# Experts worked on in the order of their number of chunks, sorted on VectorE, and a scatter that GpSimd waits for one step later

## The reference

```python
def moe_ffn(x, w_router, router_bias, w_gate, w_up, w_down):
    gates = group_limited_router(x2d, w_router, router_bias)      # 2 of 16 experts for each token
    y = jnp.zeros((bsz * t, d), jnp.float32)
    for e in range(N_EXPERTS):
        he = jax.nn.silu(x2d @ w_gate[e]) * (x2d @ w_up[e])
        y = y + gates[:, e:e + 1] * (he @ w_down[e])
    return y
x = layer_norm(DN_ALPHA * x + moe_ffn(x, ...), ln_ffn_g[l], ln_ffn_b[l])
```

## Time and profile before

| | us |
|---|---|
| median of 3 runs (lowest, highest) | 971.27 (966.42, 971.51) |
| profiled execution | 970.41 |
| its span, first to last instruction | 968.6 |
| TensorE busy | 890.6 |
| mixture of experts, layer 0 and layer 1 (first product of a chunk to the first of `add_choices`) | 200.6 to 469.3 and 680.3 to 941.3 |

### The profile page before, as it was taken

The page is one execution under the profiler, slowest core; times in us unless marked ns, Lnnn a source line. Parts: engine busy times, 40 slices in busy tenths (PEclk is TensorE's granted clock), DMA queues, the critical chain, the costliest instruction groups (busy, mean ns, idle before and its releaser), DMA issues.

```text
span 968.6 us, 15558 instructions
## 1 busy us (share of the span) xinstructions
PE 890.6 (92%) x5890; PEld 568.0 (59%) x5890; DVE 399.6 (41%) x885; ACT 253.9 (26%) x473; POOL 303.6 (31%) x261
## 2 busy tenths in 40 slices
PE   6998799799999997999999997996999999789895
PEld 5876678755555553555487776785555555445451
DVE  5997747721111111111559977368111111111126
ACT  5333741211111110111233357322111111111111
POOL 0632446222222221223335224661222222122123
PEclk9999799879999998999999998998899999999998
DMA  9761067899999999997504211869998999999962
GB/s 307 276 218 54 21 263 284 330 343 398 395 396 390 394 397 403 392 387 188 140 25 130 88 53 45 308 238 377 361 384 305 394 396 402 397 404 392 380 124 87
DMA packets 90421, 272.78 MB, mean 282 GB/s; under 512 B 8547, under 2 KB 24067, under 8 KB 89857
## 3 DMA queue, kind: packets, MB, share of 16 engines
q1 hardware_dynamic: 78368, 247.14, 66.2%
q0 software_dynamic: 12000, 24.88, 10.5%
HBM read 256.83 MB, written 21.23 MB: 287 GB/s over the span
## 4 chain that ended last, share of the span: by engine, by line
PE 63%; DVE 15%; DMA 15%; SPq 2%; issue 2%; ACT 1%; POOL 1%; DVEq 0%; POOLq 0%
PE bank L782 25%; PE bank L788 14%; PE bank L442 14%; DMA moew<-in_exp_w_down 5%; DVE bank L1167 5%; DMA w_down<-in_exp_w_down 3%; DMA w_down<-in_exp_w_wide 3%; DMA w_gate<-in_w_in 2%; PE bank L776 2%; PE bank L770 2%; DVE xTl L1136 2%; PE bank L833 2%; PE bank L829 2%; DMA moemem<-x_rows,first_tok 1%; DVE w_gate L1143 1%
## 5 line engine op out<-in xcount | busy, mean ns | idle before, releaser
L1418 DVE TENSOR_TENSOR moex<-bank,moemem 64x128 f32<-64x128 f32 x172 | 48.3, 281 | 341.9 <-ACT moemem L1045 339.2
L1584 POOL TENSOR_TENSOR wl<-w_gate,wh 128x2048 fp32r<-128x2048 f32 x17 | 77.9, 4589 | 138.4 <-ACT wh L908 98.6
L442 PE MATMUL bank<-xTh,wh 128*128 128x512 f32 (+1 forms) x256 | 101.4, 396 | 11.4 <-DVE xTl L1136 10.1
L782 PE MATMUL bank<-w_up,moex 128*64 128x256 f32 x896 | 101.5, 379 | 3.1 <-DMA w_up<-in_exp_w_wide 3.1
L1045 ACT ACTIVATE moemem<-bank 64x256 f32<-64x256 f32 x86 | 32.8, 381 | 260.8 <-PE bank L782 260.8
L442 PE MATMUL bank<-xTh,wl 128*128 128x512 f32 (+1 forms) x256 | 94.9, 371 | 0.0
L442 PE MATMUL bank<-xTl,wh 128*128 128x512 f32 (+1 forms) x256 | 94.9, 371 | 0.0
L1647 POOL COPY scatter_idx<-toki 128x1 int32 x41 | 7.6, 186 | 266.4 <-DMA y_rows<-moemem,scatter_idx 266.4
L782 PEld LDWEIGHTS bank<-w_up,moex 128*64 128x64 f32 x896 | 64.1, 137 | 41.7 <-issue 7.4
L782 PE MATMUL bank<-w_gate,moex 128*64 128x256 f32 x768 | 87.0, 379 | 1.1 <-DMA w_gate<-in_exp_w_wide 1.1
L782 PE MATMUL bank<-w_down,moex 128*64 128x256 f32 x672 | 79.8, 392 | 1.7 <-DMA w_down<-in_exp_w_wide 1.7
(11 more groups left out here) (228 smaller groups left out, 1356.3 us busy)
## 6 DMA issues: line engine op xcount, KB each, us to landing
w_up<-in_exp_w_wide SPq DMA_DIRECT2D x20, 2048.0 KB, 22.9
w_gate<-in_exp_w_wide SPq DMA_DIRECT2D x18, 2048.0 KB, 25.9
w_down<-in_exp_w_wide SPq DMA_DIRECT2D x16, 2048.0 KB, 26.5
w_down<-in_exp_w_down SPq DMA_DIRECT2D x12, 2048.0 KB, 20.7
w_gate<-in_exp_w_down SPq DMA_DIRECT2D x8, 2048.0 KB, 24.2
w_gate<-in_w_in SPq DMA_DIRECT2D x13, 1024.0 KB, 6.6
xtok<-in_exp_w_wide SPq DMA_DIRECT2D x6, 2048.0 KB, 18.1
w_up<-in_exp_w_down SPq DMA_DIRECT2D x6, 2048.0 KB, 27.0
```

The lines of the kernel that those rows point to most:

```text
L442: mm = pe.matmul(out, xs[i], ws[k], start=(first and n == 0), stop=(last and n == 2))
L782: return [pe.matmul(bank[i][CH * n:CH * n + CH, 0:256], x, w[:, 512 * n + 256 * i:512 * n + 256 * i + 256], start=(k == 0), stop=(k == KD ...
L1418: dve.tensor_tensor(he[CH * b:CH * b + CH, P * i:P * i + P], bank[i][0:CH, P * b:P * b + P], silu[:, 256 * i + P * b:256 * i + P * b + P], ...
L1584: pool.tensor_tensor(wl[(n + l) % SLOTS][:, :], wraw[n % 2], wh[(n + l) % SLOTS][:, :].bitcast(F32), ALU.subtract)\
```

## The change

Experts 0 to 3 keep their places. Experts 4 to 15 are worked on in descending order of their number of chunks (at a tie the lower number first). A position in the loops and in the ring is now a rank, not an expert's number; only SyncE has to know which expert it is, and reads it from `orderi`. A key of each expert (16 x chunks + a constant) is compared with every other on VectorE; the weighted and the plain sum of the comparisons give each expert's first chunk (`start_of`) and its rank, and a one-hot of the ranks gives the bounds of the loops and the expert of each rank. `start_set` is raised twice in a layer, first when the starts of ranks 0 to 3 stand, then for the rest.

Of GpSimd's chunk, the copy of `gather_idx` goes to VectorE (`move_gathered`), and the wait for a scatter and the copy of `scatter_idx` stand ahead of the next scatter, behind the next gather. The first chunk of a layer is taken out of the loop and issues two scatters with indices out of range.

```diff
@@ -183,7 +185,9 @@
         r4 = [scr[:, 656 + 4 * i:660 + 4 * i] for i in range(6)]
         beat = scr[:, 2048:2304].rearrange("p (g m) -> p g m", m=EG * EG)
         nch = scr[:, 680:696]
-        zero16 = scr[:, 696:712]
+        key_of, start_of, place_of, expert_at = (scr[:, 960 + E * i:960 + E * i + E] for i in range(4))
+        ahead = scr[:, 2048:2304].rearrange("p (e f) -> p e f", e=E)
+        weighed, held = (scr[:, 1536 + 256 * i:1792 + 256 * i].rearrange("p (e f) -> p e f", e=E) for i in range(2))
         place = scr[:, 712:720]
         gt = scr[:, 736:744]
         away = scr[:, 744:748]
...
@@ -331,10 +336,11 @@
                 dst = wraw[n % 2].rearrange("p (k n) -> p k n", n=src.shape[2])
                 sp.dma_start(dst, src).then_inc(wraw_in[n % 2], 16)
 
-            def load_expert(l, e, part):
-
-                src = a["exp_w_down"][l * E + e] if part == DOWN else a["exp_w_wide"][l * E + e, 512 * part:512 * part + 512, :]
-                sp.dma_start(weights(e, part), src.rearrange("(k p) n -> p k n", p=P)).then_inc(wexp_in[(3 * e + part) % R], 16)
+            def load_expert(l, e, part, at=None):
+
+                rows = slice(0, 512) if part == DOWN else slice(512 * part, 512 * part + 512)
+                src = a["exp_w_down" if part == DOWN else "exp_w_wide"][bass.ds(l * E + e if at is None else at, 1), rows, :]
+                sp.dma_start(weights(e, part), src.rearrange("o (k p) n -> p (o k) n", p=P)).then_inc(wexp_in[(3 * e + part) % R], 16)
 
             def load_rows(l):
...
@@ -418,10 +424,13 @@
                 load_expert(l, 2, DOWN)
 
                 starts = [first_chunk(sp, l, e) for e in range(1, E - 1)]
+                sp.wait_ge(order_set, l + 1)
                 for i in range(R, 3 * E):
                     e, part = (i - R) // 3, (i - R) % 3
+                    if i // 3 >= FIXED and (i % 3 == 0 or i == R):
+                        at = sp.value_load(orderi[0:1, i // 3:i // 3 + 1], min_val=l * E, max_val=l * E + E - 1)
                     sp.wait_ge((wide_half, wide_done, narrow_done)[part], starts[e] * 2)
-                    load_expert(l, i // 3, i % 3)
+                    load_expert(l, i // 3, i % 3, at if i // 3 >= FIXED else None)
 
                 sp.wait_ge(narrow_done, starts[E - 3] * 2)
                 sp.dma_start(rffn, a["rows_ffn"][l].partition_broadcast(P)).then_inc(rows_in, 16)
...
@@ -739,8 +748,8 @@
                                    start=(j == 0), stop=(j == TT - 1))
                 mm.then_inc(first_done, 1)
                 idle_products(16)
-                pe.wait_ge(start_set, l + 1)
-                starts = [first_chunk(pe, l, e) for e in range(6)]
+                pe.wait_ge(start_set, 2 * l + 1)
+                starts = [first_chunk(pe, l, e) for e in range(FIXED)]
 
                 for q in range(2 * TT):
                     if q % TT == 0:
...
@@ -748,7 +757,8 @@
                     mm = pe.matmul(bank[3][:, 0:MAXCH], hot_slot[:, q, :, :], hot_rows[:, q, :],
                                    start=(q == 0), stop=(q == 2 * TT - 1))
                 mm.then_inc(tab_done, 1)
-                starts += [first_chunk(pe, l, e) for e in range(6, 12)]
+                pe.wait_ge(start_set, 2 * l + 2)
+                starts += [first_chunk(pe, l, e) for e in range(FIXED, 11)]
                 return starts
 
             def late_tables(l):
...
@@ -805,7 +815,7 @@
                         mm.then_inc(done, 1)
                 turn_hidden(c, 0)
 
-                pe.wait_ge(xg_moved, c + 1)
+                pe.wait_ge(xg_moved, c * 2 + 2)
                 turn_gathered(l)
 
                 weights_in(pe, l, e, DOWN)
...
@@ -1060,7 +1070,7 @@
                     piece(l + 1, 0)
                     piece(l + 1, 1)
                 if not last:
-                    act.wait_ge(scattered, (c - l + 1) * 16)
+                    act.wait_ge(scattered, (c + 2) * 16)
                 result(c, 1 if last else 0)
 
             act.sem_inc(y_set, 1)
...
@@ -1096,7 +1106,7 @@
                 act.activation(ex, lg, ACT.Exp).then_inc(rt_exp, 1)
 
                 act.activation(idle[:, 1:2], eps, ACT.Silu)
-                act.wait_ge(start_set, l + 1)
+                act.wait_ge(start_set, 2 * l + 2)
                 first, end = first_chunk(act, l, 0), first_chunk(act, l, E)
                 gathered_turned(first, l)
                 with act.Fori(first, end - 1) as c:
...
@@ -1369,12 +1378,17 @@
                 link(dve.tensor_scalar(counted, cnt, float(CH - 1), None, ALU.add))
                 link(dve.tensor_scalar(counted, counted, CHLOG, None, ALU.logical_shift_right))
                 link(dve.tensor_scalar(nch, counted, 1.0, None, ALU.max))
-                link(dve.tensor_tensor_scan(startf[:, l, 1:E + 1], nch, zero16, startf[:, l, 0:1], ALU.add, ALU.add))
-                dve.tensor_copy(starti[:, l * (E + 1):(l + 1) * (E + 1)], startf[:, l, :]).then_inc(start_set, 1)
+                link(dve.scalar_tensor_tensor(key_of, nch, float(E), cst[:, K_KEY:K_KEY + E], ALU.mult, ALU.add))
+                link(dve.tensor_tensor(ahead, key_of.unsqueeze(1).broadcast_to([P, E, E]), bc3(key_of, E), ALU.is_gt))
+                link(dve.tensor_tensor(weighed, ahead, nch.unsqueeze(1).broadcast_to([P, E, E]), ALU.mult))
+                link(dve.tensor_reduce(start_of, weighed, AX.X, ALU.add))
+                link(dve.tensor_scalar(start_of, start_of, startf[:, l, 0:1], None, ALU.add))
+                base = l * (E + 1)
+                dve.tensor_copy(starti[:, base:base + FIXED], start_of[:, 0:FIXED]).then_inc(start_set, 1)
                 dve.wait_ge(first_done, l + 1)
                 dve.tensor_tensor(first_tok[:, :], bank[1][:, 0:1], cst[:, K_OFF:K_OFF + 1], ALU.add).then_inc(first_set, 1)
 
-                stb = startf[:, l, 0:E].unsqueeze(1).broadcast_to([P, TT, E])
+                stb = start_of.unsqueeze(1).broadcast_to([P, TT, E])
                 link(dve.scalar_tensor_tensor(comb.rearrange("p (j e) -> p j e", j=TT), stb, float(CH), rank,
                                               ALU.mult, ALU.add))
                 link(dve.tensor_tensor(kk2, comb.unsqueeze(1).broadcast_to([P, 2, TT * E]), oh12, ALU.mult))
...
@@ -1390,6 +1404,17 @@
                 for h in range(2):
                     at = slot_of[:, TT * h:TT * h + TT].unsqueeze(2).unsqueeze(3).broadcast_to([P, TT, 2, CH])
                     dve.tensor_tensor(hot_slot[:, TT * h:TT * h + TT, :, :], slots, at, ALU.is_equal).then_inc(rt_hot, 1)
+                link(dve.tensor_reduce(place_of, ahead, AX.X, ALU.add))
+                link(dve.tensor_tensor(held, place_of.unsqueeze(1).broadcast_to([P, E, E]),
+                                       bc3(iota[:, 0:E], E), ALU.is_equal))
+                link(dve.tensor_tensor(weighed, held, start_of.unsqueeze(1).broadcast_to([P, E, E]), ALU.mult))
+                dve.tensor_tensor(ahead, held, iota[:, 0:E].unsqueeze(1).broadcast_to([P, E, E]), ALU.mult)
+                link(dve.tensor_reduce(nch[:, 0:1], nch, AX.X, ALU.add))
+                link(dve.tensor_scalar(startf[:, l, E:E + 1], nch[:, 0:1], startf[:, l, 0:1], None, ALU.add))
+                link(dve.tensor_reduce(startf[:, l, FIXED:E], weighed[:, FIXED:E, :], AX.X, ALU.add))
+                dve.tensor_copy(starti[:, base + FIXED:base + E + 1], startf[:, l, FIXED:E + 1]).then_inc(start_set, 1)
+                link(dve.tensor_reduce(expert_at, ahead, AX.X, ALU.add))
+                dve.tensor_scalar(orderi[:, :], expert_at, float(l * E), None, ALU.add).then_inc(order_set, 1)
                 link(dve.tensor_tensor(kk2, ex.rearrange("p j e -> p (j e)").unsqueeze(1).broadcast_to([P, 2, TT * E]),
                                        oh12, ALU.mult))
                 link(dve.tensor_reduce(gt, kk2.rearrange("p r (j e) -> p (r j) e", j=TT), AX.X, ALU.add))
...
@@ -1428,6 +1453,7 @@
 
                 dve.wait_ge(gathered, c * 16)
                 dve.wait_ge(xg_turned, c + l)
+                dve.tensor_copy(gather_idx[:, :], toki[:, bass.ds(c + 1, 1)]).then_inc(xg_moved, 1)
                 dve.tensor_copy(xg, xg_next).then_inc(xg_moved, 1)
 
             def chunk(l, c):
...
@@ -1623,9 +1649,13 @@
 
             def gather(c, l):
 
-                pool.tensor_copy(gather_idx[:, :], toki[:, bass.ds(c, 1)]).then_inc(idx_set, 1)
-                pool.wait_ge(idx_set, c)
                 gather_rows(l, xg_next, gather_idx).then_inc(gathered, 16)
+
+            def scatter(l):
+
+                pool.sem_inc(scatter_sent, 1)
+                pool.indirect_dma_start(y_halves[l], bass.IndirectOffsetOnAxis(ap=scatter_idx[:, :], axis=0), ysb[0], None,
+                                        bounds_check=2 * T - 1, oob_is_err=False, compute_op=ALU.add).then_inc(scattered, 16)
 
             def gather_rows(l, to, rows):
...
@@ -1635,16 +1665,14 @@
 
             def chunk(l, c):
 
-                pool.wait_ge(xg_moved, c + 1)
```

(30 more changed lines are left out.)

3 lines of the change are left out of this document (1 added, 2 removed).

## The result

The changed kernel takes 978.79 us (median of 4 runs, 977.84 to 981.76), the kernel before 970.66 beside it: medians 8 us apart; the ratio of the runs side by side is 1.0111, 95% interval 1.0083 to 1.0139, some 11 us. Forecast was 970.0 with a range of 955 to 981 and half the chance on no change. The profiled execution of the changed kernel took 977.84 against 970.41, 7.4 us more, and it is these 7.4 us that the traces can be asked about; its span is 975.7 against 968.6.

A forecast was written before the change was run, and what follows sets the result against it. Two streams, TensorE's chunks and the DMA's weights, were taken to bound the mixtures. Layer 0's -0.8 and layer 1's -0.3, each including 4 us of router, gave -1.1 on 970.41, forecast 970, range 955 to 981.

The forecast's parts named there:

- part 3: DMA under the new order: heavy experts free slots late; x1 at 456.6 in layer 0, 934.0 in layer 1.
- the price of a part: DMA time for one part of an expert's weights in the full queue: taken as 5.6 us.
- part 4: Tails of both layers, waiting for DMA: layer 0 -0.8 us, layer 1 -0.3, the router's cost included.
- What bounds it: In the mixtures, TensorE's chunks and the DMA's weight stream; either can end the stage; weight waits 11 and 16 us.
- part 2: New order for TensorE alone, without weight waits: stage ends -7.0 us in layer 0, -11.9 in layer 1.
- Part 1: Router ahead of the chunks, longer by the added instructions: 4 us a layer, between 2.5 and 5.5.
- rival C: Ranks stay as they are for these counts, so only the router's cost acts: +8 us, 979; chance 0.03.
- rival B: Late DMA stream dearer than 5.75 us a part, weights late in layer 1: 977 or 986 us; chance 0.20.
- the ends: Layer 0's tail: -7 us if the projection's pieces come in time, +3 if adding DMAs cost them 4 us.
- Part 5: GpSimd's new chunk, VectorE's extra copy and SyncE's register reads: covered by other work, no time.

The follow-up runs named there:

- e5: Changed kernel without TensorE's seven register reads behind the second start_set, each bound read at its expert's loop: 976.28 us, ratio 1.0090 to the kernel before.
- e1: Changed kernel with constant sort keys, so the order is as before while the sort's instructions stay: 977.41 us, ratio 1.0087 to the kernel before.
- e13: Changed kernel measured again, unaltered, on another chip: 981.20 us, ratio 1.0120 to the kernel before.
- e14: Changed kernel with GpSimd's chunk, copies and waits as before, second measurement: 979.58 us, ratio 1.0105 to the kernel before.
- e6: Changed kernel without the loads of the x1 rows in layer 1: 979.44 us, ratio 1.0110 to the kernel before.
- e10: Changed kernel without layer 1's x1 rows, its adding DMAs there also held until the last expert weights land: 970.18 us, ratio 1.0026 to the kernel before.

## Why the prediction was wrong

The forecast was -1.1 us on the profiled time; it came to +7.4 (970.41 to 977.84). The steps that failed are the price of a part in part 3 (5.6 us, from a misread row; the rows of before give 5.8) and the first adding DMA of layer 0 in part 4 (5.6 us taken, 9.1 measured), and with them the 9 us that the new order was to bring. By the marks of the table above, to the first product of the results in layer 1:

| us | forecast | measured |
|---|---|---|
| up to the router of layer 0 | 0 | -1.2 |
| the two routers | +4.0, +4.0 | +4.6, +4.8 |
| chunks and tail of layer 0 | -4.8 | -2.1 |
| chunks and tail of layer 1 | -4.3 | +0.9 |
| sum | -1.1 | +7.0 |

- **What bounds it, and part 2, held.** The counts, and TensorE's chunks without waits: forecast to end at 462.3 and, measured from a first product at 684.3, 929.5; measured 460.8 and 937.4, of which 2.2 us are the later start, 0.9 the slow products and 4.2 waits for the last weights (the remaining 0.6 I can't place).
- **Part 1 was short by 1.4 us.** The routers were given 4.0 us each, the slower first chunk included, and took 4.6 and 4.8. The step that failed here is "that ends about when the gate table does": the seven register reads ended after it. `start_set` was raised at 679.3, the gate table stood at 683.2, TensorE turned the rows at 683.82 and took up the table at 684.58. Without the reads (e5) the routers cost 3.1 and 3.5, the +3.3 of the forecast. The first chunk was 1.2 us faster than before in layer 0 and 0.9 slower in layer 1; the forecast had 0.7 slower. e1, in which the ranks are those of before, is rival C of the forecast (+8): 8.4 by the ratio.
- **Part 3: the mechanism held, the price of a part was read wrong.** The DMA ran dry behind the heavy experts, as forecast. But x1's landing in the kernel before was taken as 903.3 + 18.9 = 922.2, the first of four issues with the longest of four times, and that time belongs to the last block. One line, L343 (x1 rows), kernel before, layer 1, 906.6 to 907 us:

```profile
L343 SPq DMA_DIRECT2D w_up<-x_rows x1: 1727/1727/1727, 906.6 to 906.6; - x1
DMA to landing us min/median/max: 18.9/18.9/18.9
```

So x1 landed at 925.5, and in layer 0 at 426.4 + 18.3 = 444.7 instead of 439.2. A part then cost (925.5 - 829.7) / 16.5 = 5.81 us and (444.7 - 382.4) / 10.5 = 5.93, not 5.6 and 5.4. In the changed kernel part 29 was issued at 820.25 and landed 8.3 us later, at 828.55; to the last x1 row at 940.5 are 112.0 us for 19.5 parts: 5.74. The price did not rise with the change: read rightly it was at or above rival B's 5.75 from the start. With 5.8 the forecast's own working puts x1 at 938.1 and layer 1 at +3.8 instead of -0.3 (an estimate), and rival B's case, "at 5.8 and a contended layer 0", was 977. Of the 5.2 us that layer 1's chunks and tail missed by, 2.8 are this price (112.0 against 109.2), 0.9 the first chunk, 0.8 the slow products at the end, and 0.7 of the slot and the landing of part 29 that I can't place.
- **Part 4: layer 0's end was priced in the wrong place.** I took 5.6 us for the first adding DMA from layer 1, where nothing runs beside it. In layer 0 two pieces of the projection do, and it took 9.1. From the layer's first product it landed 6.8 us later than forecast, 3.5 by this and 3.4 because x1 did (459.4, forecast 456.6). So add_choices waited for the adding DMAs (8.1 us) and ScalarE's last result, ready at 468.5, was no limit; forecast was 470.4 for it. I had this collision among the ends, but only as a cost to the pieces. That the second piece landed at 465.9, forecast 466, is luck: it was put 9.5 us behind x1, where the rows of before have 5.4 (450.1 against 444.7), and x1 came later. TensorE's idle time cost 1.8 us at each end, not 1.0.
- **Part 5 held**: GpSimd's chunk is neutral (e13, e14).

The forecast's larger fault is one of judgement: where two streams are forecast within 1 us of each other (462.3 and 462.6 in layer 0), every term that was taken too low shows up in full.

What the forecast had wrong without an effect on the number is the picture of x1 as the one link that holds the tail. It is work in a full queue: taking it out let dearer work (the adding DMAs) forward and gained nothing (e6); it gained 7.4 us only with those held back (e10).

## What to carry to other kernels

When a loop eats buffers that a saturated queue fills, an order is judged by both streams: put the long consumers where the ring is empty, not all in front, and ask what the queue still has to move when the last long one releases its slot. A wait at the end of such a queue isn't removed by removing the transfer it names alone; count the work that is left, by whom, and what overtakes what. Where one row sums up several issues and their landing times, pair each time with its own issue before a price is taken from it. Where two limits come out equal, price each term on the dear side for the stream that has the most unknown terms.

## What the hardware showed that I had not expected

An adding DMA is dear and gets ahead of plain ones. Four of 512 KB land within 5.7 to 11.4 us of issue when alone (layer 1), 9.1 to 16.0 beside the pieces, up to 20.5 beside expert weights (e6). In e6 the rate of all DMA fell from 395 GB/s at 910 to 920 us to 274 at 930 to 935, with a share of 1.05: the engines were as full as ever and moved less. With nothing beside them the adding DMAs of the changed kernel's layer 1 filled the engines (share 1.06) at 206 GB/s. Stretches of e6, then one of the changed kernel (its length, then busy time and number of instructions of PE, PE's loads, DVE, ACT and POOL, the granted clock, the DMA's share and GB/s):

```profile
910.00:920.00 10.00, 9.96 (x81) 5.55 (x77) 1.33 (x5) 2.04 (x4) 2.84 (x3) 1.00 1.03 395
920.00:930.00 10.00, 6.77 (x47) 3.19 (x45) 0.78 (x3) 0.69 (x1) 3.68 (x4) 1.00 1.04 377
930.00:935.00 5.00, 0.26 (x2) 0.26 (x4) 0.00 (x0) 0.00 (x0) 0.00 (x0) 0.68 1.05 274
```

```profile
946.00:950.00 4.00, 3.45 (x4) 1.18 (x4) 0.00 (x0) 0.00 (x0) 0.00 (x0) 0.50 1.06 206
```

The Trainium skill ("DMA: Bandwidth & Descriptors", Queues, rings and completion order) says that an engine goes round between the rings that have work. e6 agrees in that GpSimd's DMAs, issued last, delayed weights issued 14 us and more before them: the last two parts took 32.1 and 36.5 us from issue to landing, 26.9 and 26.7 in the changed kernel.

Register reads are not free on TensorE's queue: in layer 1 seven of them followed each other every 0.65 us (679.3 to 683.2), 4.5 us from the second `start_set` to the next product, and the router was 1.5 us a layer shorter without them (e5). And an engine that stands for 8 us at the end of its work pays again: the granted clock was 0.50 at 945 to 950 us in layer 1 of the changed kernel, the lower of the two levels (1.2 GHz), and four products took 3.78 us instead of 1.98.
